# Seven heads' scales applied inside the last head of an HGRN2 mixer, with their output products for three tiles behind its level products

## The reference

```python
def readout(o, g):
    o = rms_norm(o.transpose(0, 2, 1, 3), norm_g).reshape(bsz, n_tok, D_MODEL)   # per head and token
    return (o.astype(g.dtype) * jax.nn.silu(g)) @ w_out
...
x = layer_norm(ALPHA * x + mx[2] * yx, ln_g[i, 0], ln_b[i, 0])
ctx = layer_norm(ALPHA * ctx + mc[2] * yc, ln_g[i, 0], ln_b[i, 0])
```

## Time and profile before

| | us |
|---|---|
| median of 3 runs | 2875.9 |
| lowest and highest | 2867.69, 2875.99 |
| the profiled execution: its time | 2878.65 |
| its span in the profile | 2876.9 |
| TensorE busy | 2645.5 (92%) |
| VectorE busy | 2326.0 (81%) |
| mean granted clock of TensorE, share of full speed | 0.964 |

### The profile page before, as it was taken

The page is one execution under the profiler, slowest core; times in us unless marked ns, Lnnn a source line. Parts: engine busy times, 40 slices in busy tenths (PEclk is TensorE's granted clock), DMA queues, the critical chain, the costliest instruction groups (busy, mean ns, idle before and its releaser), DMA issues. The chain is left out here.

```text
span 2876.9 us, 41318 instructions
## 1 busy us (share of the span) xinstructions
PE 2645.5 (92%) x13950; PEld 2263.6 (79%) x13950; DVE 2326.0 (81%) x4250; ACT 1166.8 (41%) x2016; POOL 825.1 (29%) x565
## 2 busy tenths in 40 slices
PE   7999978899888999999999999889898779999997
PEld 3888864579777899999999999856497658888886
DVE  2788876699997777777877877855499879999999
ACT  2233320333385333333333333224344646666664
POOL 0000001325453244444333333200266441112121
PEclk9999988899999999999999999989998999999999
DMA  6223224404379998888888888720234899999996
GB/s 259 94 97 124 80 103 147 175 30 155 124 214 329 342 352 301 310 310 309 308 311 311 306 308 310 254 112 30 103 122 151 252 364 361 358 348 361 363 361 241
DMA packets 247818, 682.38 MB, mean 237 GB/s; under 512 B 20172, under 2 KB 106804, under 8 KB 244020
## 3 DMA queue, kind: packets, MB, share of 16 engines
q1 hardware_dynamic: 192436, 480.00, 46.0%
q0 software_dynamic: 55296, 201.35, 19.5%
HBM read 635.34 MB, written 45.92 MB: 237 GB/s over the span
## 5 line engine op out<-in xcount | busy, mean ns | idle before, releaser
L1120 PE MATMUL bank<-v_parts,p_parts 128*128 128x512 f32 x3072 | 743.0, 392 | 8.6 <-DVE p_parts L2034 8.6
L1120 PEld LDWEIGHTS bank<-v_parts,p_parts 128*128 128x128 f32 x3072 | 577.9, 189 | 127.3 <-issue 7.3
L1061 PE MATMUL bank<-h_parts,u_hi 128*128 128x384 f32 (+1 forms) x2048 | 511.5, 333 | 13.5 <-POOL u_lo L2281 8.4
L1061 PEld LDWEIGHTS bank<-h_parts,u_hi 128*128 128x128 f32 x2048 | 372.0, 191 | 22.8 <-issue 12.9
L2032 DVE TENSOR_TENSOR v_parts<-arena,v_parts 128x1024 fp32r<-128x1024 f32 x256 | 313.4, 1224 | 50.9 <-ACT v_parts L1509 49.4
L1061 PE MATMUL bank<-h_parts,u_lo 128*128 128x384 f32 (+1 forms) x1024 | 340.7, 333 | 0.0
L1509 ACT ACTIVATE v_parts<-arena 128x1024 fp32r<-128x1024 f32 x256 | 269.1, 1051 | 79.4 <-PE bank L1120 59.3
L2296 POOL DMA_INDIRECT arena<-in_v,arena x128 | 197.0, 1539 | 320.9 <-DVE arena L2054 297.0
L1506 ACT ACTIVATE arena<-bank 128x384 f32<-128x384 f32 x104 | 51.1, 491 | 557.8 <-PE bank L1061 557.8
L2005 DVE TENSOR_TENSOR u_lo<-arena,u_hi 128x1024 fp32r<-128x1024 f32 x208 | 253.3, 1218 | 19.1 <-ACT u_hi L1416 16.8
L1051 PE MATMUL bank<-h_parts,u_hi 128*128 128x384 f32 x832 | 245.7, 360 | 13.9 <-DVE u_lo L2005 13.7
(11 more groups left out here) (308 smaller groups left out, 4681.1 us busy)
## 6 DMA issues: line engine op xcount, KB each, us to landing
arena<-in_u SPq DMA_DIRECT2D x256, 512.0 KB
arena<-in_v SPq DMA_DIRECT2D x256, 512.0 KB
arena<-in_wm SPq DMA_DIRECT2D x80, 512.0 KB
arena<-in_wst SPq DMA_DIRECT2D x19, 2048.0 KB, 7.9
gate_scratch<-arena SPq DMA_DIRECT2D x18, 2048.0 KB, 8.7
arena<-gate_scratch SPq DMA_DIRECT2D x30, 768.0 KB
arena<-in_whd SPq DMA_DIRECT2D x8, 2560.0 KB, 9.5
arena<-gate_scratch SPq DMA_DIRECT2D x30, 384.0 KB
```

What stands on the lines that cost most here:

```text
L1061: last = mm(banks[q][:, 0:ND[p]], w[:, q, col], h[:, k, DS[p]], start=(n3 == 0), stop=(n3 == 3 * KT - 1))
L1120: last = mm(banks[2 + 2 * b + half][:, :], x[:, q, at:at + P], y[:, q, col], start=(first and i == 0), stop=(final and i == 2))
```

## The change

The 28 mean squares of heads 0 to 6 get a power of their own on GpSimd, ready as soon as head 6 is done; the four of head 7 get a second one. In the last head VectorE builds head h's diagonal behind the copy of level h + 1 and applies head h's scales behind level h + 2 (heads 0 to 5), and head 6's ahead of the states. TensorE spreads the scales behind the level products into bank 7, and behind each it multiplies one head's scaled output with the weights for three output tiles, (0, 0), (1, 0) and (0, 1): a spread alone behind level 2, a spread and three products (eight matmul instructions) behind levels 3 to 7 and behind the key transposes, three products behind the state products. The first three products wait for both transfers of `wout0`. Behind the head, seven products for the tile (1, 1) stand ahead of the turn of the modulation columns; then come head 7's scales and the rest of the output. The diagonals move to a free place in memory, and the order of the output tiles changes.

```diff
-        WOUT_ORDER = [[(0, 1), (1, 1), (0, 0), (1, 0), (2, 0), (3, 0), (2, 1), (3, 1)], [(0, 1), (0, 0), (1, 0), (1, 1)]]
+        WOUT_ORDER = [[(0, 0), (1, 0), (0, 1), (1, 1), (2, 0), (3, 0), (2, 1), (3, 1)], [(0, 1), (0, 0), (1, 0), (1, 1)]]
...
-            return ar(A_LM + TOK * (h % 2), TOK)
+            return ar(W[h % 2] + KT * WCOLS, TOK)
+
+        SPREAD = [7] * 7 + [6]
+        EARLY = 7
+        EARLY_OUT = [(0, 0), (1, 0), (0, 1)]
+        WAIT_OUT = [(1, 1)]
...
+            def spread_scale(h):
+                pe.wait_ge(rdiag, h + 1)
+                if h == 0:
+                    pe.wait_ge(vsb, 2 * HEADS)
+                elif h < EARLY:
+                    pe.wait_ge(onorm, h)
+                mm(banks[SPREAD[h]][:, :], mean_w, rmsdiag(h), start=True, stop=True).then_inc(rbc, 1)
+
+            def early_outputs(k):
+                if k == 0:
+                    arrived("wout0", 0)
+                    arrived("wout0", 1)
+                pe.wait_ge(onorm, k + 1)
+                for b, half in EARLY_OUT:
+                    out_part(b, half, k)
...
                     last.then_inc(lvl, 1)
+                    if not more and l >= 2:
+                        spread_scale(l - 2)
+                        if l >= 3:
+                            early_outputs(l - 3)
...
                     last.then_inc(kt_pe, 1)
+                if not more:
+                    spread_scale(6)
+                    early_outputs(5)
...
                     last.then_inc(ds, 1)
...
+                if not more:
+                    early_outputs(6)
...
+            arrived("wout0", 1)
+            for k in range(EARLY):
+                for b, half in WAIT_OUT:
+                    out_part(b, half, k)
             pe.wait_ge(mod_c, 2)
             for s in range(2):
                 last = nc.tensor.transpose(banks[7][0:32, s * P:(s + 1) * P], modcol[:, 0, 32 + s:96:2], ident)
             last.then_inc(mod_t, 1)
-            for h in range(HEADS):
-                pe.wait_ge(rdiag, h + 1)
-                mm(banks[h % 4][:, :], mean_w, rmsdiag(h), start=True, stop=True).then_inc(rbc, 1)
+            spread_scale(EARLY)
             pe.wait_ge(onorm, HEADS)
             pe.wait_ge(modT_a, 1)
-            mixer_out("wout0", oT, WOUT_ORDER[0])
+            for b, half in WOUT_ORDER[0]:
+                for k in range(EARLY if (b, half) in EARLY_OUT + WAIT_OUT else 0, KT):
+                    last = out_part(b, half, k)
+                last.then_inc(y_pe, 1)
...
                     if l in (1, 3, 5):
                         mod_sum(h, 2 + l // 4, (l // 2) % 2)
+                    if not more:
+                        scale_diagonal(l - 1)
+                        if l >= 2:
+                            scaled(l - 2)
...
+            def scale_diagonal(h):
+                if h == 0:
+                    dve.wait_ge(rms_p, 1)
+                if h >= 2:
+                    dve.wait_ge(rbc, h - 1)
...
+            def scaled(h):
+                dve.wait_ge(rbc, h + 1)
+                V.tensor_tensor(oT[:, h, :], banks[SPREAD[h]][:, :], oT[:, h, :], ALU.mult).then_inc(onorm, 1)
...
                 levels(h, slot, more, more2)
+                if not more:
+                    scaled(EARLY - 1)
                 states(h, slot)
...
+            dve.wait_ge(rms_p, 2)
+            scale_diagonal(EARLY)
+            scaled(EARLY)
...
-            pool.wait_ge(ms_a, 1 + HEADS)
-            ms = stat[:, 0:HEADS * NB]
-            G.tensor_tensor(ms, ms, neg_half.broadcast_to([P, HEADS * NB]), ALU.pow).then_inc(rms_p, 1)
+            for h0, h1 in ((0, EARLY), (EARLY, HEADS)):
+                pool.wait_ge(ms_a, 1 + h1)
+                ms = stat[:, h0 * NB:h1 * NB]
+                G.tensor_tensor(ms, ms, neg_half.broadcast_to([P, (h1 - h0) * NB]), ALU.pow).then_inc(rms_p, 1)
```

More of the change, by code:

```diff
@@ L885, in _, with out_part @@
             value_piece(0, 0, KT)
+            def out_part(b, half, k):
+                last = mm(banks[2 * b + half][:, :], oT[:, k, b * P:(b + 1) * P], wt(RING[("wout0", half)] % 2)[:, k, :],
+                          start=(k == 0), stop=(k == KT - 1))
+                return last
+            def spread_scale(h):
[12 more added lines that the diff above has]
+                    out_part(b, half, k)
             def head(h, slot, more):
@@ L1719, in levels @@
                         mod_sum(h, 2 + l // 4, (l // 2) % 2)
+                    if not more:
+                        scale_diagonal(l - 1)
+                        if l >= 2:
+                            scaled(l - 2)
                 if more2:
                     low_w(h + 2, slot, 0)
+            def scale_diagonal(h):
[3 more added lines that the diff above has]
+                    dve.wait_ge(rbc, h - 1)
+                V.tensor_tensor(rmsdiag(h).rearrange("p (b t) -> p b t", b=NB), ident.unsqueeze(1).broadcast_to([P, NB, P]),
+                                stat[:, h * NB:(h + 1) * NB].unsqueeze(2).broadcast_to([P, NB, P]), ALU.mult).then_inc(rdiag, 1)
+            def scaled(h):
+                dve.wait_ge(rbc, h + 1)
+                V.tensor_tensor(oT[:, h, :], banks[SPREAD[h]][:, :], oT[:, h, :], ALU.mult).then_inc(onorm, 1)
             def states(h, slot):
```

## The result

The median of 7 runs is 2885.86 us (2881.31 to 2890.88) against 2875.9 us before (7 runs by then). The ratio on record is 1.0042, interval 1.0032 to 1.0052; it is estimated from the runs together with its interval, and is not the quotient of the two medians, which is 1.0035. The forecast was 2886 in a range of 2873 to 2896, slower by more than 0.3% with a chance of 0.58. The profiled execution of the changed kernel took 2890.02 us, its span is 2888.2.

The account below looks back on a forecast made before the run. It took the last head's chain, then VectorE's sums hanging on transfers, as the bound, not TensorE's output products. Block 34's 10.0 us on 2878.65 gave 2888.7 profiled; the median, 2.75 lower, 2886, range 2873 to 2896.

Parts of the forecast that it names:

- A new wait on the output weights behind level 3, level 4 at 421.8: TensorE, last head: first three products wait for wout0, landing 417.5, run mostly at half clock; level 4 starts 5.6 us late.
- the prediction's own lower bound: Last head: if the clock rises before 417.5, the first group costs 2.6 us and the head grows by 5.9.
- Levels of 4.4 us at full clock from there, level 7 at 435.0, head output to 450.0: TensorE, last head: never idle from level 4 on, so priced at full clock; the head becomes 7.7 us longer.
- The power of 28 columns in 5.0 us and hidden: GpSimd, last head: runs 397.3 to 402.3, wanted by VectorE at about 408.1, so costs nothing.
- The case by which a busy VectorE draws it out to 14 us: GpSimd's 28-column power beside a busy VectorE ends at 411.4; the chain loses 3.3 us, sum 2889.
- The turn 12.4 us late, at 457.7: TensorE behind the head: longer head plus 14 instructions (6.0 us) delay the turn of the modulation columns from 445.27.
- Block 32 at 464.4, block 34 at 479.0 with some 9 us of idle time in front: Weight blocks for VectorE's sums: block 32 +1.6 us; block 34, queued behind the norm's rows landing at 477.8, +10.0 us.
- Everything behind it shifted alike, the output products no bound: From block 34 on the old rhythm, fronts start at 497.1; output products done at 491, no wait.
- The second transfer of the query weights goes out earlier: Transfer that waited for the last output tile goes out earlier; costed at nothing.
- The first rival: Norm's row transfers share engines and don't hold up block 34: landed by 470.6, +1.6 us, 2877.5, no change; chance 0.25.
- The rival by which the filled gaps pay: Extra work nearly fits idle time, head at most 4 us longer, block 34 not held up; some 2874; chance 0.07.
- The rival of half clock throughout: TensorE at half clock through the last head: levels 8.4 us, head 33 us longer, some 2917; chance 0.06.

## Why the prediction was right

The mechanism came as forecast, and most positions within 1 us. That 2886 met the median to 0.14 us is luck: the runs of the changed kernel lie 9.6 us apart, and the rest of the span behind the norm took the same time within 0.9 us in these two profiled executions, while over all ten it varied by almost 12. Step by step, with the prediction's values first, in the positions of the profile:

- *A new wait on the output weights behind level 3, level 4 at 421.8*: landing 417.5 against 417.9, level 4 at 422.3. Right. The clock went another way than told: it was at 2.4 GHz by level 3's product already (1.13 us), was still granted in full up to 417.9 while TensorE waited for the weights, fell to 0.50 as the first group began, and rose again at about 421.5; the group took 4.51 us. Most of the group at half clock is what the prediction had, but not by this way, and it was partly luck: in the run with four rows earlier, the same code on TensorE, level 3's product ran at half clock (2.04 us), the group at full clock (2.81), and level 4 started 1.9 us earlier. That is the prediction's own lower bound. The table by stretch of the changed kernel, granted clock third from the end:

```profile
404.00:410.00 6.00, 2.54 (x9) 2.21 (x10) 5.34 (x9) 1.17 (x2) 0.00 (x0) 0.54 0.89 343
410.50:414.00 3.50, 2.71 (x11) 1.26 (x10) 3.34 (x8) 0.63 (x1) 0.00 (x0) 0.88 1.00 426
...
420.50:452.00 31.50, 30.60 (x128) 18.20 (x126) 17.47 (x35) 3.36 (x6) 0.00 (x0) 0.98 0.00 1
```

- *Levels of 4.4 us at full clock from there, level 7 at 435.0, head output to 450.0*: 435.75 and 450.48. The granted clock was 1.00 from 426 to 452 us. I had said that VectorE is not the bound; once it was, by 0.21 us, behind level 6.
- *The power of 28 columns in 5.0 us and hidden*: 5.06 us, from 397.62 to 402.68, and VectorE's first diagonal ran at 408.20 with no wait. The case by which a busy VectorE draws it out to 14 us did not come. The one of four columns took 1.40 us instead of about 1; VectorE waited 0.25 us for it, and TensorE, busy until 458.17, did not.
- *The turn 12.4 us late, at 457.7*: 458.17, 12.9 late.
- *VectorE through with the scales 2.9 us earlier*: 2.7.
- *Block 32 at 464.4, block 34 at 479.0 with some 9 us of idle time in front*: 465.26 and 479.76, idle 9.10.
- *Everything behind it shifted alike, the output products no bound*: first front 10.8 us late, no wait for a tile; the last normalisation at 538.46 is 10.4 us late. The output products ended at 491.4, forecast 491. The span grew by 11.3; the last 0.9 us are not assigned.
- *The second transfer of the query weights goes out earlier*: no. It was issued at 521.3 and before at 518.2, since it stands behind block 47, which was late. It cost nothing that the timeline shows: the first query product started at 545.79 against 535.43, 10.4 us late like the norm.

The first rival, rows that don't hold up block 34, fell: 11.84 us from issue to use, and 5.3 us less with half of the rows out of the way. The rival by which the filled gaps pay fell too: the head became 8.1 us longer, and the products with their wait lengthen it by 10.4 us. The rival of half clock throughout fell with the granted clock of 1.00.

What the prediction did not see is how much of the loss could be had back. The two halves of the change differ: the scales inside the head cost no time (0.9988), while both places for products delay the turn, the 21 in the head and the 7 ahead of the turn, for work that was not on the path to begin with.

## What to carry to other kernels

In these runs an engine's idle time inside a chain was free for filler only as long as the filler was shorter than each gap, had its operands there, and stood behind, not ahead of, whatever another queue waited for. Before moving work past a small step, ask who waits for that step: here a turn of 0.4 us starts ten transfers of 512 KB, and the next block that is needed stands at the end of that queue. When an engine is made to finish earlier, the transfers that used to drain beside it have to be moved as well; either change alone was worth 0.12% and nothing, both together 0.36%.

## What the runs showed of the hardware

- Transfers of 512 KB and 2 MB that one engine issued, each over all 128 partitions, landed in the order of issue, and a late one waited for the earlier ones: 11.84 us from issue to use for a block behind 4 MB of rows, 3.56 us for one whose rows had landed at its issue. The Trainium skill, page "DMA: Bandwidth & Descriptors", section "Queues, rings and completion order", says that a later descriptor may finish its write before an earlier one. No run here showed a transfer that overtook another.
- Light filler went with a higher clock: with one spread per level, two instructions, TensorE's mean granted clock from level 2 to the head output was 0.82, 0.80 and 0.87 in the three kernels with spreads and no products, against 0.50, 0.52 and 0.52 in the three with the head of the kernel before. The head output started 30.1, 30.3 and 29.1 us behind level 2, against 30.9 in all three, although work was added. At which level the clock rose and fell differed between executions of the same code.
- Without any filler the clock of the head output differed too: 20 instructions took 3.99 us in the profiled execution before and 2.50 in the two others with that head, whose end lay at 34.9, 33.4 and 33.4.
- A power on GpSimd took 5.74 us for 32 columns, 5.06 for 28, 1.40 for 4, and for one column 0.54 or about 1.5; VectorE was busy beside the one of 28. What makes the difference for one column is not shown.
